# Layer entries and routing of a hybrid decoder trunk in another order

## What is computed

```python
for l in range(2):
    h = rmsnorm(x, attn_norm[l])
    parts = split(h @ w_in[l])            # 1024 x 3600, with 16 gate columns (mi, mf, ff) among them
    x = x + concat(hgrn2(parts), mlstm(parts), fox(parts)) @ w_out[l]
    h = rmsnorm(x, ffn_norm[l])           # x * inv_rms(x) * gain
    if l == 0: x = x + (silu(h @ w_gate) * (h @ w_up)) @ w_down
    else:
        logits = h @ router               # 1024 x 8
        top_val, top_idx = top_k(logits, 2); gates = softmax(top_val)
        x = x + sum of the two chosen experts' SwiGLU(h) * gate
return rmsnorm(x, final_norm)
```

## Time and profile before

| | us |
|---|---|
| median of three runs | 1504.29 |
| lowest and highest | 1502.01, 1504.61 |
| the profiled execution | 1504.51 |
| its span, first to last instruction | 1502.7 |
| first instruction to first projection half done | about 30 |
| dense mixer ends | about 360 |
| last residual of the second layer to the first expert piece | 515 to 537 |
| expert jobs, eight | 537 to about 1490 |

### The profile page before, as it was taken

One profiled execution on the slowest core, in us unless ns is written; L12 is line 12 of the kernel. 1 busy time (PEld: TensorE's weight loads), 2 busy tenths in 40 slices (PEclk: granted clock), 3 DMA queues, 4 the chain that ended last, 5 costly groups with the idle time before them and its releaser, 6 DMA issues.

```text
span 1502.7 us, 20849 instructions
## 1 busy us (share of the span) xinstructions
PE 1469.8 (98%) x7854; PEld 1250.3 (83%) x7854; DVE 1179.8 (79%) x933; ACT 971.5 (65%) x891; POOL 153.2 (10%) x131
## 2 busy tenths in 40 slices
PE   6999999999999999999999999999999999999997
PEld 6978899998987888888888888888888888888876
DVE  4875654545685688888888889888888888888896
ACT  4456444444556457777777777777777777777764
POOL 5121100000120261000000000000000000000480
PEclk9999999999999999999999999999999999999999
DMA  9533866643333469999999999999999999999992
GB/s 261 190 130 101 303 212 222 227 152 131 126 113 113 140 260 396 396 382 397 378 376 388 383 373 383 387 371 380 393 373 374 394 374 373 394 370 371 398 390 111
DMA packets 210263, 450.19 MB, mean 300 GB/s; under 512 B 12932, under 2 KB 37032, under 8 KB 210216
## 3 DMA queue, kind: packets, MB, share of 16 engines
q1 hardware_dynamic: 209064, 445.35, 81.5%
q0 software_dynamic: 1152, 4.19, 0.7%
HBM read 435.36 MB, written 14.16 MB: 299 GB/s over the span
## 4 chain that ended last, share of the span: by engine, by line
PE 93%; DVE 2%; ACT 2%; issue 1%; DMA 0%; POOL 0%; SPq 0%; DVEq 0%; POOLq 0%; ACTq 0%
PE bank L1593 28%; PE bank L1595 28%; PE bank L1594 27%; PE bank L2019 2%; DVE low L1439 1%; PE bank L1706 1%; DMA gain<-in_attn_norm_dram 0%; PE bank L2007 0%; PE bank L1607 0%; PE bank L1744 0%; PE bank L1772 0%; ACT XN L785 0%; PE bank L1682 0%; PE bank L1678 0%; ACT high L1041 0%
## 5 line engine op out<-in xcount | busy, mean ns | idle before, releaser
L1439 DVE TENSOR_TENSOR low<-raw,high 128x2048 fp32r<-128x2048 f32 x336 | 775.5, 2318 | 108.8 <-ACT high L1041 108.6
L1041 ACT CAST high<-raw 128x2048 fp32r<-128x2048 f32 x336 | 644.0, 1917 | 180.6 <-PE bank L1595 180.6
L1593 PE MATMUL bank<-high,xeh 128*128 128x512 f32 x896 | 353.9, 395 | 2.7 <-DVE low L1439 2.7
L1595 PE MATMUL bank<-high,xel 128*128 128x512 f32 x896 | 349.6, 390 | 0.0
L1594 PE MATMUL bank<-low,xeh 128*128 128x512 f32 x896 | 348.9, 389 | 0.0
L1593 PEld LDWEIGHTS bank<-high,xeh 128*128 128x128 f32 x896 | 168.3, 188 | 37.5 <-DVE low L1439 3.9
L1595 PEld LDWEIGHTS bank<-high,xel 128*128 128x128 f32 x896 | 168.2, 188 | 35.8
L1594 PEld LDWEIGHTS bank<-low,xeh 128*128 128x128 f32 x896 | 168.4, 188 | 33.7
L1593 PE MATMUL bank<-high,hdh 128*128 128x512 f32 x448 | 175.2, 391 | 1.4 <-DVE low L1439 1.4
L1595 PE MATMUL bank<-high,hdl 128*128 128x512 f32 x448 | 174.4, 389 | 0.0
L1594 PE MATMUL bank<-low,hdh 128*128 128x512 f32 x448 | 174.4, 389 | 0.0
(11 more groups left out here) (335 smaller groups left out, 2021.2 us busy)
## 6 DMA issues: line engine op xcount, KB each, us to landing
raw<-in_moe_w_gate_dram SPq DMA_DIRECT2D x112, 1024.0 KB, 7.8
raw<-in_moe_w_up_dram SPq DMA_DIRECT2D x112, 1024.0 KB, 8.1
raw<-in_moe_w_down_dram SPq DMA_DIRECT2D x112, 1024.0 KB, 7.7
ring<-in_w_in_dram SPq DMA_DIRECT2D x10, 2048.0 KB
dring<-in_dense_w_gate_dram SPq DMA_DIRECT2D x5, 2048.0 KB
dring<-in_dense_w_up_dram SPq DMA_DIRECT2D x5, 2048.0 KB
dring<-in_dense_w_down_dram SPq DMA_DIRECT2D x5, 2048.0 KB
ring<-in_w_in_dram SPq DMA_DIRECT2D x8, 1024.0 KB, 7.2
```

Of the source, the lines that this page charges most:

```text
L1041: act.copy(high[:, q % SPLIT, :], raw[:, q % RAW, :]).then_inc(s_hi, 1)
L1439: dve.tensor_tensor(low[:, q % SPLIT, :], raw[:, q % RAW, :], high[:, q % SPLIT, :].bitcast(F32), ALU.subtract).then_inc(s_lo, 1)
L1593: pe.matmul(o, xh, wh, start=first, stop=False)
L1595: return pe.matmul(o, xl, wh, start=False, stop=last)
```

## The change

- SP issues the gain row and the first 1 MB of the first slab ahead of the gate weights. Eight rows more are loaded with the parameter rows: the second layer's ffn gain.
- The gate biases have one semaphore for each layer instead of one for both.
- POOL makes the rounded identity third, not thirteenth; fillers use it alone. 18 fillers stand ahead of the first layer's transposes, 2 between the token tiles and 4 behind them in both layers. The 14 ahead of the ranks become 6, the 5 in the router go.
- The gate products are done by token tile: in the first layer tile 0 ahead of projection half 0, tile 1 between its two column tiles; in the second layer one after each column tile. ACT and DVE cast the gate weights later, to fit.
- The router is multiplied by the ffn gain once (DVE, in the first layer). In the second layer PE transposes X itself, not XN; logits are formed from it, and DVE multiplies them by the inverse rms when it takes them from PSUM, in bank 6 instead of 7. ACT copies three transposed banks before the last square sum.
- DVE takes the low part of piece 0 in two halves behind the choice, and those of the first tokens and pieces 1 and 2 ahead of the places.

```diff
-    GAP_NORM, GAP_DENSE, GAP_CHOICE = 10, 6, 14
+    GAP_NORM, GAP_DENSE, GAP_CHOICE = 10, 6, 6
+    GAP_START, GAP_TURN, GAP_ENTRY = 18, 2, 4
...
-        NROWS = DEPTH * CK * 4 + 4
+        GAINS0 = DEPTH * CK * 4 + 4
+        NROWS = GAINS0 + KD
...
-        s_par = sem("gate_params_loaded")
+        s_par = [sem(f"gate_params_loaded{l}") for l in range(DEPTH)]
+        s_rwg = sem("router_scaled")
...
@@ sync (SP) @@
             for t in range(T):
                 sp.dma_start(X[:, t, :], x[0, t * P:(t + 1) * P, :]).then_inc(s_x[t], 16)
+            gain_row(0)
+            w0 = ring[:, slot_of[0] * SLOT:(slot_of[0] + 1) * SLOT].rearrange("p (k n) -> p k n", k=KD)
+            sp.dma_start(w0[:, :, 0:HW], w_in[0].rearrange("(k p) n -> p k n", p=P)[:, :, HF0:HF0 + HW]).then_inc(s_w0, 16)
             gate_weights(0)
-            gain_row(0)
...
+                        sp.dma_start(PR[GAINS0:NROWS, :], ffn_norm[1, :].rearrange("(k p) -> k p", p=P)).then_inc(s_rows, 16)
@@ gpsimd (POOL) @@
             select(ident[:, :], ALU.not_equal, [[-1, P]], 0, 1, 1.0)
+            pool.wait_ge(s_cst, n[0])
+            done(pool.tensor_copy(identr[:, :], ident[:, :]))
...
-            done(pool.tensor_copy(identr[:, :], ident[:, :]))
@@ scalar (ACT) @@
-                if not l:
-                    gate_weights_high(0)
                 for t in range(T):
                     for n in range(2):
                         turned_copy(2 * l, hTh, t, n)
                 if not l:
+                    gate_weights_high(0)
                     weights_high(0, 0)
...
-                for t in range(T):
+                for t, n in ((0, 0), (0, 1), (1, 0)):
+                    square_sum(2 * l + 1, t, n)
+                if l:
                     for n in range(2):
-                        square_sum(2 * l + 1, t, n)
-                for t in range(T):
-                    for n in range(2):
-                        turned_copy(2 * l + 1, dst, t, n)
+                        turned_copy(2 * l + 1, dst, 0, n)
+                    turned_copy(2 * l + 1, dst, 1, 0)
+                square_sum(2 * l + 1, 1, 1)
+                if l:
+                    turned_copy(2 * l + 1, dst, 1, 1)
...
@@ vector (DVE) @@
-                if not l:
-                    gate_weights_low(0)
                 for t in range(T):
                     for n in range(2):
                         turned_low(2 * l, hTh, hTl, t, n)
+                    if not l and not t:
+                        gate_weights_low(0)
...
-                dve.wait_ge(s_par, NPAR)
+                dve.wait_ge(s_par[l], 16 * 3)
...
+                    if l == 0 and k == 7:
+                        dve.wait_ge(s_rw, 16)
+                        dve.wait_ge(s_pc, 1)
+                        dve.tensor_tensor(RW[:, :, :], RW[:, :, :], bc(PC[:, GAINS0:NROWS].unsqueeze(2), [P, KD, NE]),
+                                          ALU.mult).then_inc(s_rwg, 1)
...
-            piece_low(0, 0)
...
             dve.wait_ge(s_lg, 1)
-            then(dve.tensor_copy(RT[:, 0, :], ps[7][:, 0:16]))
+            dve.wait_ge(s_rms, 2 * T * 4)
+            then(dve.tensor_tensor(row(0), ps[6][:, 0:16].rearrange("p (t e) -> p t e", t=T),
+                                   bc(st[:, 3, 1, :].unsqueeze(2), [P, T, NE]), ALU.mult))
...
+            piece_low(0, 0, 0, PIECE // 2)
             dve.wait_ge(s_rk, 1)
...
             select(0, lambda t: first_slot[:, t:t + 1])
+            piece_low(0, 0, PIECE // 2)
...
             dve.tensor_scalar(jobs[:, 17:18], JB[:, 1, 15:16], -1.0, None, ALU.add).then_inc(s_jl, 1)
+            tokens_low(0, (0,))
+            piece_low(0, 1)
+            tokens_low(0, (1,))
+            piece_low(0, 2)
             dve.wait_ge(s_rx, 1)
...
-            tokens_low(0)
-            for q in range(1, SPLIT):
-                piece_low(0, q)
@@ tensor (PE) @@
-                    pe.matmul(ps[bank][:, :].rearrange("p (c s) -> p c s", c=2), identr[:, :],
-                              NM[:, :].unsqueeze(1).to_broadcast([P, 2, 2 * P]), start=True, stop=True)
+                    pe.matmul(ps[bank][:, :].rearrange("p (c s) -> p c s", c=4), identr[:, :],
+                              identr[:, :].unsqueeze(1).to_broadcast([P, 4, P]), start=True, stop=True)
...
-                pe.wait_ge(s_xn, 4 * i + 2 * t + n + 1)
+                if i == 2 * DEPTH - 1:
+                    pe.wait_ge(s_res, 8 * (DEPTH - 1) + 2 * t + n + 1)
+                else:
+                    pe.wait_ge(s_xn, 4 * i + 2 * t + n + 1)
+                rows_ = X if i == 2 * DEPTH - 1 else XN
... project_first
                 pe.wait_ge(s_hTh, 8 * l + 4)
+                if not l:
+                    gate_products(l, 0)
                 pe.wait_ge(s_wih, NCAST * l + 1)
...
-                ins.then_inc(s_pp, 1)
+                    if f == 1:
+                        ins.then_inc(s_pp, 1)
+                    if l or not f:
+                        gate_products(l, f if l else 1)
... router_logits
-                pe.wait_ge(s_rw, 16)
-                pe.wait_ge(s_res, 12)
-                pe.wait_ge(s_hT, 2 * t + 2)
+                pe.wait_ge(s_rwg, 1)
+                pe.wait_ge(s_res, 10)
                 for k in range(KD):
-                    ins = pe.matmul(ps[7][:, t * NE:(t + 1) * NE], hT[:, k, t * P:(t + 1) * P], RW[:, k, :],
+                    if k % 4 == 0:
+                        pe.wait_ge(s_hT, 2 * t + k // 4 + 1)
+                    ins = pe.matmul(ps[6][:, t * NE:(t + 1) * NE], hT[:, k, t * P:(t + 1) * P], RW[:, k, :],
... main program
-            pe.wait_ge(s_cst, 2)
+            pe.wait_ge(s_cst, 3)
             for l in range(DEPTH):
-                if l:
-                    keep_running(0, GAP_DENSE)
+                keep_running(0, GAP_DENSE if l else GAP_START)
                 for t in range(T):
                     for n in range(2):
                         turn(2 * l, t, n)
-                gate_products(l)
+                    keep_running(0, (GAP_TURN, GAP_ENTRY)[t])
                 project(l, 0)
...
-                    keep_running(0, GAP_NORM // 2)
+                    turn(2 * l + 1, 1, 0)
                     router_logits(0)
+                    turn(2 * l + 1, 1, 1)
                 else:
                     keep_running(0, GAP_NORM)
-                for n in range(2):
-                    turn(2 * l + 1, 1, n)
+                    for n in range(2):
+                        turn(2 * l + 1, 1, n)
```

More of the change, by code:

```diff
@@ L460, in bass_hybrid_trunk_kernel @@
         consts = []
-        NPAR = 16 * 3 * DEPTH
         RT_CHOSEN = 13
@@ L516, in columns @@
                 for c0, n in pieces:
-                    if u == 0:
-                        done, inc = (w_loaded[s], LOADED) if at else (s_w0, 16)
-                    else:
-                        done, inc = w_loaded[s], LOADED // len(pieces)
+                    if u == 0 and at == 0:
+                        at += n
+                        continue
+                    done, inc = w_loaded[s], LOADED if u == 0 else LOADED // len(pieces)
                     sp.dma_start(slot(u, KD, total)[:, :, at:at + n], wr[:, :, c0:c0 + n]).then_inc(done, inc)
@@ L1434, in _, with piece_low, tokens_low @@
                             add_residual(t, n)
-            def piece_low(j, q):
+            def piece_low(j, q, c0=0, c1=PIECE):
                 dve.wait_ge(s_hi, nth_piece(j, q))
-                dve.tensor_tensor(low[:, q % SPLIT, :], raw[:, q % RAW, :], high[:, q % SPLIT, :].bitcast(F32),
-                                  ALU.subtract).then_inc(s_lo, 1)
-            piece_low(0, 0)
+                ins = dve.tensor_tensor(low[:, q % SPLIT, c0:c1], raw[:, q % RAW, c0:c1], high[:, q % SPLIT, c0:c1].bitcast(F32),
+                                        ALU.subtract)
+                if c1 == PIECE:
+                    ins.then_inc(s_lo, 1)
+            def tokens_low(j, banks=(0, 1)):
+                for b in banks:
+                    dve.wait_ge(s_xh, 2 * j + b + 1)
+                    dve.tensor_tensor(xel[:, 4 * b:4 * b + 4, :], ps[2 + b][:, :].rearrange("p (c s) -> p c s", c=4),
+                                      xeh[:, 4 * b:4 * b + 4, :].bitcast(F32), ALU.subtract).then_inc(s_xl, 1)
             def select(j, rows):
@@ L1925, in _ @@
                     pe.matmul(ps[0][:, 0:2], ident[:, :], UO[:, 0:2], start=True, stop=True).then_inc(s_used, SPLIT)
-                    keep_running(0, GAP_NORM // 2)
+                    turn(2 * l + 1, 1, 0)
                     router_logits(0)
+                    turn(2 * l + 1, 1, 1)
                 else:
                     keep_running(0, GAP_NORM)
-                for n in range(2):
-                    turn(2 * l + 1, 1, n)
-                if l == 0:
+                    for n in range(2):
+                        turn(2 * l + 1, 1, n)
                     def down(i):
```

41 lines of the change are left out of this document (19 added, 22 removed).

## The result

The changed kernel takes 1487.02 us (median of 4 executions, 1486.33 to 1489.22) against 1503.18 for the kernel before on the same chip (1502.01 to 1504.61, 4): ratio 0.9896, 95% interval 0.9884 to 0.9907, some 16.2 us. The two profiled executions have spans of 1484.6 and 1502.7 us; they differ by 18.1. The page's chain is still TensorE's, with one point more of DVE; ACT still waits for PE to use its high parts, 160.6 us where the earlier trace rows had 162.3.

The account below looks back on a forecast made before the run. The prediction took TensorE's own work (93% of the span) as the bound, with gains only in both entries and the routing: −6.6 − 2.4 − 6.0 = −15.0 on 1504.5, so 1489.5 us, range 1486 to 1493.

Parts of the forecast that it names:

- First entry: First layer's start: earlier gain row, fillers and gates by tile bring the first half's evacuation sooner; −6.6 us (−2.5 to −8).
- late gate weights: First entry: gate weights queue behind the half slab and may land at 11 to 16 us; 0.5 us charged.
- the second slab: First entry: slab 1, needed by the next casts at 23.5 us, is in with about 2 us to spare.
- Second entry: Second layer's start: gates after each column tile let projection 1 begin sooner; −2.4 us (0 to −3), if the clock holds.
- the 0.3 expected to be given back: Second entry: half 2's low part is ready at 381.7 us, while projection 1 ends at 381.4; 0.3 lost.
- Routing: Last residual to piece 3: transposing X and moving piece 0's low part start routing and gather sooner; −6.0 us (−3.7 to −7.5).
- The wait before piece 3: Routing: DVE becomes the tighter engine, its low part ready at 540.3 us, PE at 539.6; PE waits 0.7.
- The clock wasn't lost: Rival, both entries: PE falls to 1.2 GHz, first entry wins 1.3 us, second nothing; 1497.2 us; 17%.
- Gate weights weren't late: Rival, first entry: gate weights land at 15 to 16 us, so the entry wins only 3; 1493 us; 12%.
- The weight stream: Rival, expert jobs: weight stream bounds them, so piece 0's low part freeing the first buffer sets the end; 1497 us; 4%.
- ninth job: Rival, routing: rounding turns a choice and puts an expert over 128 tokens, adding a job of 119 us; 1608 us; 3%.
- the body absorbed nothing: Rival, first layer's body: a slab's arrival or the like holds it to old times, routing wins little; 1502 to 1504 us; 3%.

Follow-up runs that it names:

- e3: The changed kernel with the gate weights' two transfers issued ahead of the gain row and the slab again: 1490.01 us, ratio 0.9925.
- e1: The changed kernel without the 18 fillers ahead of the first layer's transposes: 1488.73 us, ratio 0.9908.
- e2: The changed kernel with both tiles' gate products together ahead of projection half 0 in both layers, fillers kept: 1492.16 us, ratio 0.9931.
- e7: The changed kernel with the places ahead of the low parts of the first tokens and of pieces 1 and 2 again: 1487.08 us, ratio 0.9895.
- e5: The changed kernel with piece 0's low part whole and ahead of the routing operations again: 1490.53 us, ratio 0.9918.
- e6: The changed kernel with 14 fillers instead of 6 behind the logits, ahead of the ranks: 1487.31 us, ratio 0.9901.
- e8: The changed kernel with piece 3's low part also moved ahead of the places: 1487.98 us, ratio 0.9899.
- e10: The changed kernel with PE transposing the normalised XN for the router again, router not scaled, ACT's old order: 1494.03 us, ratio 0.9942.
- e12: The changed kernel with 14 fillers behind the logits, piece 3's and 4's low parts and the second job's slot clearing ahead of the places: 1485.38 us, ratio 0.988.
- e9: The kernel before with only the rounded identity made third and 22 fillers ahead of its first transposes: 1501.99 us against 1502.07, ratio 0.9995.
- e11: The changed kernel without the 18, the 2 and the 4 fillers of the entries: 1489.07 us, ratio 0.9906.

## Why the prediction was right

The forecast was 1489.5 on a profiled 1504.5, a fall of 15.0 us; the medians fell by 16.2, and 15.0 (a ratio of 0.990) lies inside the measured interval. The mechanisms were the ones named; two terms were too small, by 1.25 and 0.6, and the third was right to 0.1.

**First entry, −6.6 forecast, −7.85 measured.** The gain row was put at 8.4 and came at 7.98; in the ten other kernels that issue it first the first normalisation began at 7.42 to 8.50, so 8.4 was as good a figure as 7.98. The first transposes were put at 9.2 (8.79), the gates of tile 0 at 13.2 (12.78), their end at 15.1 (14.56), the evacuation at about 23.1 (22.39). The start gives 0.4 of it and two groups of gates, 1.8 and 1.7 rather than 1.9, some more. The 0.5 charged for late gate weights was not needed: they were expected near 12.0 for a cast at 12.4 and landed at 11.6 for a cast at 12.00. One step was wrong in the other direction: the second slab, given 2 us to spare, landed 0.4 late for ACT. The step took only the bytes in the queue, the same in either order; but SP was held for 4.26 us in the issue of the gate weights and issued the slab at 13.58, where it had at 12.13. PE was busy with the second half then, and nothing was lost.

What the prediction ascribed to this entry, e3 and e1 take apart in part: the transfer order is worth 2.2 us (e3) and the 18 fillers 1.9 (e1). In e1, e2 and e3 a fall of the clock under the first tile costs 1.5 more, but e7 has that fall with nothing taken out, so it is not shown that row order, fillers or gates by tile prevent it. That the clock held in the profiled execution was then in part luck: of the seven profiled kernels that have this entry unedited (changed, e5, e6, e7, e8, e10, e12) one lost it.

**Second entry, −2.4 forecast, −3.02 measured.** The first column tile begins 6.10 behind the fillers (forecast 6.2), each group of gates takes 1.71 rather than 1.9, twice 0.2, and the 0.3 expected to be given back was 0.07. The clock was 1.00 throughout, as the forecast needed; e2 shows that the place of the gates is the reason, and here the traces leave no doubt, eleven against three.

**Routing, −6.0 forecast, −5.90 measured.** First operation 4.7 sooner (4.6), selection 6.3 (5.9). The gather was left at its old time and took 5.27 (5.47). The wait before piece 3 was 1.42, not 0.7: DVE, the tighter engine as forecast, had the same queue, but PE reached piece 3 sooner. It is DVE's sum that set piece 3, as the forecast had it: put at 540.3, 25.34 behind the residual, it came at 25.47. e5 and e10 price its two parts: DVE's low part ahead of the routing is 2.9 us by its direct delay and 4.3 in the trace, transposing XN instead of X 2.6 and 4.1. The rest of each is clock, and 1.3 of such loss is seen in e1 without an edit. e7 shows that one named gain, the tokens' low parts ahead of the places, is no gain by itself.

**The rivals.** The clock wasn't lost in the profiled execution, though e7 shows how near that is: with the same entry it fell to 0.50 for some microseconds, behind the gates and not at the transposes, at a price of 1.5 rather than the 5.3 of this rival. Gate weights weren't late. The weight stream wasn't the bound, there was no ninth job (336 casts of pieces, 8 times 42), and the body absorbed nothing.

**What the forecast lacked.** The dips of 1.4 us in the levels. They are the difference between 16.8 and 18.1, and with the falls in e7's entry and in the routings of e1 and e8 they set how well any comparison here can be made.

What stays open is e9, why a profiled gain of 3.5 us doesn't show in ten timed executions; what opens the clock in the first entry, where e11 and the kernel before differ; and what of e1's, e2's and e3's loss there is the edit's.

## What to carry to other kernels

Where PE comes out of a pause into narrow matmuls, put dense ones between the narrow groups rather than only ahead of them: in the second entry fillers ahead of 32 narrow products did not save the clock, 24 wide products between two groups of 16 did. A transfer of many tiny rows should stand behind the small one that everything waits for (2.2 us here). Before a slow group is put down to an edit, look for the same group in kernels whose edit lies elsewhere: e7's entry and e1's routing were slow with nothing changed. Where two engines are close to level, as DVE and PE before piece 3, a faster PE (e6) or another order of DVE's work (e7, e8) only moves the wait: look at the sum of work ahead of the point that counts, and move out of it what that point doesn't need (e12).

## What the runs showed of the hardware

Behind sixteen float32 transposes, with no other work ahead of them, PE ran at full speed in e11 and at half of it in the kernel before. In the profile the granted clock reads 1.00 before the first change that it records even where PE ran at the slow spacing: from 8 to 12 us in e11 the transposes took 3.38 us for 16, 0.21 each, beside a clock of 1.00. There the duration of a group is to be believed, not the clock.

```profile
10.00:12.00 2.00, 2.00 (x12) 1.85 (x10) 1.95 (x3) 1.47 (x3) 1.73 (x5) 1.00 0.62 91
```

And the clock dips in the levels, 0.8 to 0.9 for 5 to 10 us and some 1.4 us of time each, come in the traces of some kernels and not in those of others with the same code there. So do the fall in the first entry (e7) and the early one in the routing (e1).
